# A mixture of experts in fp32: the weights of the last 768 inner columns become the stationary operand

## The reference, cut to what matters

```python
xe = xt[idx]                                   # (16, cap, 1024)
hid = jax.nn.silu(jnp.einsum('ecd,edf->ecf', xe, w_gate)) * jnp.einsum('ecd,edf->ecf', xe, w_up)
ye = jnp.einsum('ecf,efd->ecd', hid, w_down) * g[..., None]
out = jnp.zeros_like(xt).at[idx.reshape(-1)].add(ye.reshape(-1, D))
```

## Time and profile before

| | |
|---|---|
| median of the runs | 1912.24 us (1911.2 to 1912.28) |
| span of the profiled execution | 1910.2 us; no other time of that execution is given |
| PE matmuls, weight loads (PEld) | 1880.5 us (98%), 892.3 us (47%), 16685 of each |
| DVE, ACT, POOL | 28%, 16%, 7% |
| DMA | 644.66 MB in all, mean 337 GB/s |
| chain that ended last | PE 95%, DVE 2%, DMA 2% |

### The profile page before, as it was taken

The page is one execution under the profiler, slowest core; times in us unless marked ns, Lnnn a source line. Parts: engine busy times, 40 slices in busy tenths (PEclk is TensorE's granted clock), DMA queues, the critical chain, the costliest instruction groups (busy, mean ns, idle before and its releaser), DMA issues.

```text
span 1910.2 us, 36676 instructions
## 1 busy us (share of the span) xinstructions
PE 1880.5 (98%) x16685; PEld 892.3 (47%) x16685; DVE 534.2 (28%) x971; ACT 298.4 (16%) x544; POOL 141.7 (7%) x222
## 2 busy tenths in 40 slices
PE   6999999999999999999999999999999999999998
PEld 3999888889833333333333333333333333333332
DVE  3687466656362010101101110101101110110114
ACT  4322355543310000000000000000000000000001
POOL 2000000000211000101000010101000010100004
PEclk9999999999999999999999999999999999999999
DMA  9744111123489999999999999999999999999996
GB/s 357 301 159 168 56 48 45 64 108 119 167 328 423 419 425 421 416 427 419 426 419 425 419 425 416 417 415 419 418 419 419 412 419 417 418 420 419 420 407 261
DMA packets 63011, 644.66 MB, mean 337 GB/s; under 512 B 7536, under 2 KB 10112, under 8 KB 22416
## 3 DMA queue, kind: packets, MB, share of 16 engines
q1 hardware_dynamic: 55392, 618.38, 77.9%
q0 software_dynamic: 6608, 20.85, 3.4%
q10 hardware_dynamic: 864, 3.15, 0.4%
HBM read 625.83 MB, written 16.52 MB: 336 GB/s over the span
## 4 chain that ended last, share of the span: by engine, by line
PE 95%; DVE 2%; DMA 2%; issue 0%; POOL 0%; ACT 0%; POOLq 0%; SPq 0%; DVEq 0%; ACTq 0%
PE ps L997 93%; PE ps L1178 1%; DVE m_dump L1990 1%; DMA xn_dram<-xq 1%; DMA xe<-xn_dram,idx_g 0%; DMA m_half<-in_w_mod_rows 0%; DMA x<-in_x_sample 0%; PE ps L1005 0%; PE ps L1100 0%; PE ps L1307 0%; DVE in_lo L1966 0%; DVE Gs L2051 0%; PE ps L1201 0%; PE ps L1034 0%; POOL rsx L844 0%
## 5 line engine op out<-in xcount | busy, mean ns | idle before, releaser
L997 PE MATMUL ps<-ring,xeT 128*32 128x512 f32 (+1 forms) x9216 | 914.2, 557 | 2.1 <-DVE xeT L2330 2.1
L997 PEld LDWEIGHTS ps<-ring,xeT 128*32 128x32 f32 x9216 | 298.8, 110 | 609.7 <-issue 605.3
L997 PE MATMUL ps<-ring,hidT 128*32 128x512 f32 x3840 | 418.0, 592 | 0.0
L2427 DVE TENSOR_TENSOR hid<-sil,ps 128x768 f32<-128x768 f32 (+1 forms) x48 | 42.6, 887 | 897.6 <-ACT sil L1831 897.6
L997 PEld LDWEIGHTS ps<-ring,hidT 128*32 128x32 f32 x3840 | 124.9, 110 | 283.7 <-issue 283.7
L1831 ACT ACTIVATE sil<-ps 128x768 f32<-128x768 f32 (+1 forms) x48 | 36.3, 757 | 955.7 <-PE ps L997 955.1
L997 PE MATMUL ps<-hT_hi,gq_hi 128*128 128x320 f32 x256 | 86.5, 338 | 0.0
L997 PE MATMUL ps<-in_hi,hT_hi 128*128 128x384 f32 x240 | 82.3, 343 | 0.1
L997 PE MATMUL ps<-in_lo,hT_hi 128*128 128x384 f32 x240 | 80.5, 335 | 0.0
L997 PE MATMUL ps<-in_hi,hT_lo 128*128 128x384 f32 x240 | 80.3, 335 | 0.0
L997 PE MATMUL ps<-hT_hi,gq_lo 128*128 128x320 f32 x256 | 79.1, 309 | 0.0
(11 more groups left out here) (278 smaller groups left out, 1522.4 us busy)
## 6 DMA issues: line engine op xcount, KB each, us to landing
ring<-in_w_gu SPq DMA_DIRECT2D x128, 2048.0 KB, 23.3
ring<-in_w_dn SPq DMA_DIRECT2D x80, 2048.0 KB, 18.0
ring<-in_w_gu_rest SPq DMA_DIRECT2D x64, 1536.0 KB, 18.9
last_block<-in_w_dn_last SPq DMA_DIRECT2D x16, 1024.0 KB, 19.3
m_half<-in_w_mod_rows SPq DMA_DIRECT2D x12, 1024.0 KB, 5.6
in_slab<-in_w_in_blocks SPq DMA_DIRECT2D x6, 1536.0 KB, 6.5
gq<-in_w_gates SPq DMA_DIRECT2D x16, 512.0 KB, 3.6
slab<-in_w_mod_blocks SPq DMA_DIRECT2D x3, 2048.0 KB, 16.0
```

The source lines that it names most:

```text
L997: return pe.matmul(out, lhsT, rhs, start=first, stop=last, **kw)
L2427: dve.tensor_tensor(hid[:, :, 0:n], sil[:, :, 0:n], ps[:, b:b + 3, n:2 * n], ALU.mult).then_inc(hid_ready, 1)
```

## The change

The third inner part (768 columns) is computed the other way round. The weights become the stationary operand, 128 rows by 32 inner columns, and the 80 tokens stream through (`xeT[:, k, 0:CT]`). Per chunk k there are 2 halves (gate, up) * 6 blocks of 128 columns * 4 column tiles = 48 matmuls of 128 x 80. The result has inner columns on partitions and tokens in columns: gate in PSUM bank 0, up in bank 1, 6 * 80 = 480 columns each. ACT and DVE work on 128 x 480 instead of 128 x 576, and the product is `hid2`, stationary for the down matmuls as it is: `turned(e, 2)` goes, and the down of part 2 waits for `hid_ready`. The host lays the weights of that part out in another order; loads, their number and sizes are as before, and so are the down matmuls, except that the third group writes 16 rows instead of 32 in the context ones.

```diff
     both = np.stack([np.asarray(w_gate)[0], np.asarray(w_up)[0]]).reshape(2, E_, KD, P, FF)
     wide = both[..., 0:2048].reshape(2, E_, KD, P, 2, 4, 256).transpose(1, 4, 2, 3, 5, 0, 6)
-    rest = both[..., 2048:].reshape(2, E_, KD, P, 4, 192).transpose(1, 2, 3, 4, 0, 5)
+    rest = both[..., 2048:].transpose(1, 2, 3, 0, 4)
...
-        hidT = [at(f"hidT{i}", E0 + 17408 + i * 3072, [P, 3, GW[i]]) for i in range(NGRP)]
+        hidT = [at(f"hidT{i}", E0 + 17408 + i * 3072, [P, 3, GW[i]]) for i in range(2)]
+        sil2, hid2 = at("sil2", E0 + 11264, [P, NL2, CT]), at("hid2", E0 + 17408 + 2 * 3072, [P, NL2, CT])
...
+            def gate_up_turned(e):
+
+                pe.wait_ge(hid_ready, val(e, NGRP, 1))
+                for k in range(KD):
+                    w = arrived(("gu", number(e), 2, k))
+                    for half in range(2):
+                        for f in range(NL2):
+                            for x in range(4):
+                                c0 = half * NL2 * P + f * P + 32 * x
+                                last = mm(ps[32 * x:32 * x + 32, half, f * CT:(f + 1) * CT], w[:, c0:c0 + 32],
+                                          xeT[:, k, 0:CT], k == 0 and f == 0, k == KD - 1 and f == NL2 - 1)
+                    last.then_inc(w_used, 1)
 
             def down(e, G):
 
-                pe.wait_ge(hidT_ready, val(e, NGRP, G + 1))
+                if G == 2:
+                    pe.wait_ge(hid_ready, val(e, NGRP, 3))
+                else:
+                    pe.wait_ge(hidT_ready, val(e, 2, G + 1))
                 if G == 0 and not is_first(e):
                     pe.wait_ge(yr_ready, val(e, 2, 0))
+
+                def inner(G, b, g):
+                    if G == 2:
+                        return hid2[:, b, 32 * g:min(32 * g + 32, CT)]
+                    return hidT[G][:, g, 32 * b:32 * b + 32]
...
                 down(e, 0)
-                gate_up(e, 2)
+                gate_up_turned(e)
                 down(e, 1)
                 down(e, 2)
...
-                b = group_bank(G)
-                act.activation(sil[:, :, 0:GW[G]], ps[:, b:b + 3, 0:GW[G]], ACT.Silu).then_inc(sil_ready, 1)
+                if G == 2:
+                    out, gate = sil2[:, :, :], ps[:, 0, 0:NL2 * CT].rearrange("p (f t) -> p f t", f=NL2)
+                else:
+                    b = group_bank(G)
+                    out, gate = sil[:, :, 0:GW[G]], ps[:, b:b + 3, 0:GW[G]]
+                act.activation(out, gate, ACT.Silu).then_inc(sil_ready, 1)
...
                 dve.wait_ge(sil_ready, val(e, NGRP, G + 1))
+                if G == 2:
+                    up = ps[:, 1, 0:NL2 * CT].rearrange("p (f t) -> p f t", f=NL2)
+                    dve.tensor_tensor(hid2[:, :, :], sil2[:, :, :], up, ALU.mult).then_inc(hid_ready, 1)
+                    return
...
                 gated(e, 2)
-                turned(e, 2)
```

More of the change, by code:

```diff
@@ L47 @@
 GD = (8, 8, 6)
+NL2 = GD[2]
 CL = 2 * LAT // E_
@@ L148, in down_blocks @@
     w, blocks, r = np.asarray(w_down)[0], [], 0
-    for n in GW:
+    for n in GW[:2]:
         blocks.append(w[:, r:r + 4 * n].reshape(E_, 4, n // 32, 32, D).transpose(0, 2, 1, 3, 4).reshape(E_, n // 32, P, D))
         r += 4 * n
+    blocks.append(w[:, r:].reshape(E_, NL2, P, D))
     blocks = side_by_side(np.concatenate(blocks, 1))
@@ L1404, in gate_up @@
                         pe.wait_ge(x_add, val(e, 2, 3))
-                    if k == 0 and G == 2:
-                        pe.wait_ge(hid_ready, val(e, NGRP, 1))
-                    elif k == 0 and not is_first(e):
+                    if k == 0 and not is_first(e):
                         pe.wait_ge(hid_ready, val(e, NGRP, 0 if G == 0 else -1))
@@ L1427, in latents @@
                             h0 = i * D + x // 2 * 512
-                            last = mm(ps[32 * x:32 * x + 32, 3, :], hidT[G][:, x % 2, 32 * (c + i):32 * (c + i) + 32],
+                            last = mm(ps[32 * x:32 * x + 32, 3, :], inner(G, c + i, x % 2),
                                       w[:, h0:h0 + 512], first and i == 0, last_ and i == 1)
@@ L1434, in context @@
                     for x in range(4):
-                        last = mm(ps[32 * x:32 * x + 32, 4, :], hidT[G][:, 2, 32 * (c + x // 2):32 * (c + x // 2) + 32],
-                                  w[:, x * 512:x * 512 + 512], first, last_)
+                        there = inner(G, c + x // 2, 2)
+                        rows = CC if G == 2 else 32
+                        last = mm(ps[32 * x:32 * x + rows, 4, :], there, w[:, x * 512:x * 512 + 512], first, last_)
                     return last
@@ L2423, in gated @@
                 dve.wait_ge(sil_ready, val(e, NGRP, G + 1))
+                if G == 2:
+                    up = ps[:, 1, 0:NL2 * CT].rearrange("p (f t) -> p f t", f=NL2)
+                    dve.tensor_tensor(hid2[:, :, :], sil2[:, :, :], up, ALU.mult).then_inc(hid_ready, 1)
+                    return
                 if G > 0 or not is_first(e):
-                    dve.wait_ge(hidT_ready, val(e, NGRP, G))
+                    dve.wait_ge(hidT_ready, val(e, 2, G))
                 n, b = GW[G], group_bank(G)
@@ L2489, in _ @@
             gated(last, 2)
-            turned(last, 2)
             for i in range(2, NT):
```

## The result

The changed kernel takes **2164.87 us** (median of 4 runs, 2160.70 to 2169.28) beside 1912.26 for the kernel before (4 runs, 1911.20 to 1913.06). The ratio is 1.1323, with a 95% interval of 1.1309 to 1.1336. The forecast was 1910.3 us in a range of 1902 to 1918: wrong by 254.6 us. The mechanism is the one of rival D, which had 6% and a price of 1974 us.

The account below looks back on a forecast made before the run. PE was taken as the bound by a hair, with nearly full DMA engines close behind. Terms -11.0 + 4.7 + 3.1 + 1.3 = -1.9 us gave 1910.3 us from 1912.24, range 1902 to 1918.

Parts of the forecast that it names:

- rival D: Third part: PE runs out of instructions, each packet costing it 1 us; stage 19.5 us, total 1974; chance 6%.
- The bound, the lead: Expert loop: PE bounds by a hair; loaded weights lead by 11.0 us, all that faster matmuls can take away.
- The round of 80 columns, 69.5 ns: Third part: a round of four column-tiled matmuls of 80 columns takes an estimated 69.5 ns.
- rival C: Third part: instruction, not column, sets PE's rate; 98 ns per round, stage 19.0 us, total 1966; chance 14%.
- PE's part of the forecast: Third part: 192 rounds take 13.5 us against 15.66, 2.1 us less per expert, 34 us in all.
- (a): DMA engines: 72 more instruction packets beside the weights delay the last landing by 4.7 us (2.8 to 7).
- (b): Last expert: `fin` loads and POOL's gathers come before the last block, delaying its landing 3.1 us (1.6 to 4).
- (c): Kernel's end: SP's stores wait behind weights, delaying the context scatter and POOL's last step 1.3 us (0 to 3).
- What would show it: Changed profile: 12288 matmuls, 203 packets, third part 13 to 14 us, DMA `ring` waits from about expert 6.

Follow-up runs that it names:

- quarters' kernel: Changed kernel with two column tiles of 64; in experts 0 to 14 two third-part chunks alternate with two down pairs: 1909.97 us, ratio 0.9996.
- the idle case: Changed kernel with weight loads of experts 2 to 15 cut to 256 of 4096 columns: 2005.39 us; kernel before, same cut: 1911.98.

## Why the prediction was wrong

**The bound, the lead: right.** In the quarters' kernel the lead is used up, and PE waits 10.8 us for DMA in all. The lead of 11.0 us is what is won at most, and most of it is given back.

**The round of 80 columns, 69.5 ns: right.** Rounds in a burst start 69.5 ns apart. The rule of the Trainium skill (TensorE: Matmul & The Clock Gate, "Wait — 56ns, not 53.3ns?") that starts are never under about 25 ns apart, which I weighed as 100 ns per round (rival C), is not borne out for four column tiles: 128 matmuls, 32 rounds, take 2.42 us, 19 ns a start.

**The step that failed** is in PE's part of the forecast: "The stage then has 8 * 48 * 2 = 768 instructions, 192 rounds: 192 * 69.5 + 0.2 = 13.5 us". It puts PE's wait for its instructions at nothing, and part (a) charges the 72 packets to the DMA engines alone. Measured are 11.2 us of such waits in a part that takes 30.5. Rival D named the wait, but mis-sized it too: "A packet takes 1.04 us and queues behind weights. If each costs PE 1 us, the stage takes 19.5". 1.04 us is how long a packet's transfer takes; 1.07 us is measured for it in the idle case. What counts for PE is how far apart two packets are: 3.4 to 4.1 us with idle engines, mostly about 6 in full queues. I had both numbers for the comparison, 6 packets and 13.5 us, 2.25 us per packet, and compared them with the transfer instead of the distance. The trace before could not show the distance, since PE never waited there for a packet: its closest two start 9.2 us apart, so it bounded the distance from above by 9.2 us and not by 1, and the chance of D should have been of the size that such a bound gives. Priced with the distances of the part shown above (5.6 us on average from 1108.68 to 1130.97), 5 further packets make about 28 us; 30.5 are measured.

**The clock** had no term at all. In the changed kernel 19.3 us busy per part less 13.5 is 5.8 us, most of it bursts at the lower level (0.16 us of each burst's length is its end), a third of the 16 to 17 us that a part loses against my 13.5. In the rows shown, gaps of 2.15, 2.48 and 2.98 us were followed by the lower level, gaps of 0.54 to 1.96 us were not; the counts over the whole trace are above.

**The other terms**, measured on the quarters' kernel, which has 24 more packets rather than 72. First landings of experts 2 and 15 are 699.6 and 1805.7, 85.08 us per expert against 84.76 before: (a) is +4.5 us by expert 15, not the 1.6 of 24 packets. Some of that may come from the other order of loads and the deeper queue; this was not separated. The last block is first used at 1894.05, 9.0 us after its landing before (1885.0), so what is left for the part around the `fin` loads (b) is +4.5 rather than +3.1. It is found by difference and not measured by itself; the last block is issued at 1853.62 there, before the `fin` loads at 1858.40, and still takes 40.4 us to land beside them. From there to the end of the span it is 14.15 us (1908.2 - 1894.05), as it was 14.13 (1910.2 - 1896.07): (c) is 0, not 1.3. The sum -11.0 + 4.5 + 4.5 = -2.0 equals the 2.0 us by which the profiled span is shorter, but as (b) is the remainder, this is no check of it. The changed kernel itself spends none of this, since its weights wait for PE.

**What would show it**, as I wrote it: 12288 matmuls and 203 packets came true; no DMA wait on PE and a stage above 15.4 us were to prove me wrong, and did.

**Open:** what the 2.4 us from a packet's start to PE's first matmul consist of (1 is transfer), and whether the distance of packets would shrink with other loads beside it (smaller pieces, fewer engines). No version tried beats the kernel before by more than can be measured: where the instructions are in time, PE waits for weights at the DMA engines' bound.

## What to carry to other kernels

Count instructions per microsecond before making matmuls smaller, loads of the stationary operand included. Here 256 of them need about 3.5 us beside idle DMA engines and about 6 beside full ones, or 14 and 23 ns per instruction. Beside full queues dense stretches of 768 instructions cost gaps of up to 2.1 us, stretches of 384 ten gaps of up to 1.1 us in the whole run, stretches of 192 none. A dense stretch can be thinned without any other change by moving other work of the same engine into it, preferably work with the same tile shape; and idle time put down to "issue" that recurs after a fixed number of instructions is the mark of it.

## What the runs showed of the hardware that I had not expected

- PE's instructions come through the DMA engines beside the weights: 256 per packet, to all appearance one under way at a time, 3.4 to 4.1 us apart with idle DMA engines, mostly about 6 with full ones. Making the weights the stationary operand in tiles of 32 columns multiplies the instructions; the orientation by itself shows no cost, and the count of instructions made the kernel 13% slower.
- In the rows shown, idle times of 2.15 to 2.98 us on PE were followed by bursts of 3.6 to 3.9 us mostly at 1.2 GHz (0.57 and 0.62 granted). Of the changed kernel's gaps that began at the upper level, 27 of 31 of 2.5 us or more were followed by a lower clock, none of the 11 under 2 us.
- A change between column tiles of 64 and of 32 and back costs about 0.28 us (4.52 against 4.24 us, and 8.76 against 8.49); between two uses of tiles of 32, with the sides turned, nothing was seen.
